# Hybrid mixer and mixture-of-experts layer on one core: where the cache rows are turned and stored, and the order of work between the output projection and the first expert product

## The chip, the cores and the metric

The kernel runs on one core of a Trainium2 chip. The metric is the device time of one execution in microseconds (us), as the median of several runs.

## What is computed

One decoder layer for a prompt of 256 tokens and a sample group of 8 x 4 tokens, T = 288 rows of D = 1024 in fp32, and a final norm.

```
xn   = rmsnorm(x) * g_mix
proj = xn @ w_in                       # columns: B gate | C gate | h | v, 512 each
u    = C * h;  z_c = B * dwconv3(u)    # last 2 rows of u per sequence are outputs (new_conv)
z_p  = scale * GroupLinear(trailing_mean_w(v) - v), w in (2, 4, 8, 16)
                                       # last 15 rows of v per sequence are outputs (new_pool)
x1   = x + concat(z_c, z_p) @ w_out
xf   = rmsnorm(x1) * g_ffn
logits = xf @ router_w + router_b;  top 4 of 32;  gates = softmax(top 4)
for e in 32 experts:  gu = xf @ w1[e] + b1[e];  gate = min(gu_left, 7);  lin = clip(gu_right, -7, 7)
                      x1 += gates[:, e] * ((gate * sigmoid(1.702 * gate) * (lin + 1)) @ w2[e] + b2[e])
y    = rmsnorm(x1) * g_final
```

The experts' weights are 32 x 12.6 MB, about 400 MB in all, and each is read once.

## The kernel before

Every engine has its own program with semaphores between them. The order of the work is written out by hand. TensorE's program goes through these stages.

**Input projection (L567 to L628).** x is turned onto partitions. Each of x and w_in is split into a high part (ACT, L955) and a low part (DVE for x, POOL for w_in, L1540), and one block (128 rows of w_in by 512 columns) is 4 x 3 products of 128x128 by 288 columns (L625 to L627). There are four groups of 8 blocks: v, C, h, B, into banks 4 to 7, 0 to 3, 4 to 7, 0 to 3. ACT may be three blocks ahead at most (`w_mix_used`). At block 0 of the second group TensorE broadcasts the rms factor over partitions by products of ones with a diagonal (L594); DVE copies it out (L1245) and then scales v, forms the trailing sums (L1262 to L1272) and C (L1277). When h is done, DVE makes u (L1282) and the convolution (L1291 to L1297). At block 2 of the last group (L599 to L606) TensorE turns the last rows of u and v, the caches, into banks 4 to 7; ACT copies them to `cache_rows` (L987 to L990) and issues 11 stores between its high parts (L1006). At block 6 TensorE makes the four pool products (L613, L614), after `cache_read`, since they write the same banks.

**Output projection (L631 to L649).** 16 blocks of the same kind, w_out's low part from POOL (L1546). As the columns of x1 are done, DVE adds x (L1334, `x1_ready`) and ACT squares (L1027, `x1_sq_ready`).

**Router (L652 to L660).** For each of 8 column blocks m of x1, one product with the router's weights (L656), written to partition group m % 3 of bank 7, and one of ones with the squares (L659), always to partition group 3. They are fp32. ACT copies the partial sums (L1029) and six small products with `pick_logits` (L673) add up the groups and turn them.

**Gate and first gather (L662 to L688, L892 to L900).** TensorE turns x1 back to rows (L666) into the banks of `TURNED_BANKS`. ACT copies the left half (L1033), and scales it into x_norm, three tiles of the left half, then exp, then copy, then three of the right half (L1036, L1047). DVE makes logits, the top 4, `mask`, then waits for exp, makes `combine` with its reciprocal, waits for the ranks (TensorE, L682, L684), and makes rank and `place`, the one-hot matrix of slots of a pair of experts. `gather_first` (L714) picks the rows of a pair by products with `place`: three pieces of 2, 2 and 4 column blocks (`FIRST_PIECES`). ACT copies each with the gain (L1056, `first_read`).

**Experts.** They go in 16 pairs, 64 slots for each expert of a pair, one period of each engine's program per pair. A period has 8 first products (L757; 4 units i of two j) for its own pair, and 2 units of second products (L779) for the pair before it; a unit is 4 MB in one of four ring slots. `add_b1` (L692) and `add_b2` (L700) start the banks with the biases, `turn_back` is L736, `gather` L710, `turn_gathered` L728, `turn_hidden` L745, and spreading back to tokens is L801 and L802. Each unit's last product signals `used`, and SyncE's queue loads a slot again when its unit has been used (L427 for w1, L432 for w2). In the first two pairs nothing is spread back; pair 1's period has the first second products (198.99 us in the trace), then ACT's `high_y` and DVE's `low_y` (L1420). `work` is one scratch buffer: `cache_rows` lies where `y_low` is written.

The change moves lines of these functions; what it touches follows with the line numbers of the profile.

Of the kernel before, what the change touches and what calls it, by code (L numbers as in the profile page):

```python
# [53 lines left out]
def hybrid_moe_layer(nc, x_prompt, x_sample, state_conv, state_pool, norm_mix_g, w_in, conv_w,  # L54
# [30 lines left out]
    with ctx:  # L85
# [129 lines left out]
        last_at = KD * T  # L215
        u_last = flat_n[:, last_at:last_at + KC * NB * CB].rearrange("p (k n) -> p k n", k=KC)
        v_last = flat_n[:, last_at + KC * NB * CB:last_at + KC * (NB * CB + NS)].rearrange("p (k n) -> p k n", k=NG)
        assert last_at + KC * (NB * CB + NS) <= NTILE * D

# [15 lines left out]
        FIRST_PIECES = ((0, 1), (2, 3), (4, 5, 6, 7))  # L235
        FIRST_BANKS = (7, 6, 4)
# [287 lines left out]
        def _(pe):  # L524
            mm = nc.tensor.matmul

            def keep_awake(times, moving):

                for _ in range(times):
                    mm(psum[:, 6, 0:moving.shape[-1]], ident[:], moving, start=True, stop=True)  # L530
# [22 lines left out]
            for j in range(4):  # L553
# [8 lines left out]
                for k in range(KD):  # L562
# [27 lines left out]
                    if j == 1 and k == 0:  # L590
# [6 lines left out]
                    if j == 3 and k == 2:  # L597


                        pe.wait_ge(last_ready, 1)  # L600
                        for i in range(KC):
                            nc.tensor.transpose(psum[0:CB, 4, i * P:(i + 1) * P], u_pad[:, i, NP:NP + CB], ident[:])
                            nc.tensor.transpose(psum[0:NB * CB, 5, i * P:(i + 1) * P], u_last[:, i, :], ident[:])
                            nc.tensor.transpose(psum[0:PB, 6, i * P:(i + 1) * P], v_pad[:, i, NP:NP + PB], ident[:])
                            last = nc.tensor.transpose(psum[0:NS, 7, i * P:(i + 1) * P], v_last[:, i, :], ident[:])
                        last.then_inc(cache_ready, 1)  # L606
                    if j == 3 and k == 6:

                        pe.wait_ge(pooled, 1)
                        pe.wait_ge(cache_read, 1)  # L610
# [19 lines left out]

            pe.wait_ge(z_pool_low_ready, NG)  # L631
            for i, (k, n) in enumerate(OUT_BLOCKS):
# [16 lines left out]
                last.then_inc(w_mix_used, 1)  # L649


            pe.wait_ge(router_ready, 1)  # L652
            for m in range(KD):
                pe.wait_ge(x1_ready, max(m + 1, KC))
                g = m % 3
                mm(psum[g * E:(g + 1) * E, 7, 0:T], router_g[:, m, :], x1_t[:, m, :], start=(m < 3), stop=(m >= KD - 3),  # L656
                   skip_group_check=True)
                pe.wait_ge(x1_sq_ready, m + 1)
                last = mm(psum[3 * E:4 * E, 7, 0:T], ones[:, 0:E], x1_sq[:, m, :], start=(m == 0), stop=(m == KD - 1),  # L659
                          skip_group_check=True)  # L660
# [17 lines left out]
            for t in REST_ORDER:  # L678
                turn_x1(1, t)

# [6 lines left out]
            def add_b1(h, b):  # L687

                pe.wait_ge(picked_b1, 2 * h + b + 1)
                for c in range(W1N):  # L690
# [58 lines left out]
            def first_product(h, b, i, j, first=False):  # L749
# [5 lines left out]
                for c in range(W1N):  # L755
                    for e in range(2):
# [47 lines left out]
            def period(h, b, first=False, spreads=True, final=False):  # L804
# [8 lines left out]
                else:  # L813
                    add_b1(h, b)
# [3 lines left out]
                for i in range(2):  # L818
                    for j in range(2):
                        first_product(h, b, i, j, first)  # L820
# [3 lines left out]
                        if second and i + j == 0:  # L824
                            pe.wait_ge(gt_read, 2)
                            turn_hidden(h, b)
                        if direct and j == 1 and i == 0:
                            pe.wait_ge(x_norm_ready, NTILE + 1)
                            pe.wait_ge(x_rest_copied, 1)
                            gather_first(1)  # L830
                            pe.wait_ge(first_read, 2)
                        if direct and i == 1 and j == 0:
                            pe.wait_ge(x_norm_ready, 2 * NTILE)
                            pe.wait_ge(x_rest_copied, NTILE)
                            gather_first(2)
# [5 lines left out]
                if direct:  # L841
                    pe.wait_ge(first_read, 3)
# [739 lines left out]
```

## Time and profile before

| | us |
|---|---|
| median of 3 runs | 1062.56 (1062.09 to 1066.23) |
| the profiled execution | 1058.53 |
| its span, first to last instruction | 1056.8 |
| TensorE busy / its weight loads | 999.4 / 414.0 |
| VectorE (DVE) busy | 290.3 |
| ScalarE (ACT) busy | 175.9 |
| GpSimd (POOL) busy | 75.4 |
| HBM read / written | 418.62 MB / 1.49 MB |

A row of the timeline gives the start in us, the duration, engine, line and operation, out<-in, and how many records it merges; in brackets the idle time before it and what ended it. A product in fp32 leaves two records, one in the split form (fp32r) and a transpose leave one. PE is TensorE, PEclk its granted clock as a share of 2.4 GHz. SPq is the queue on which SyncE issues loads.

### The profile page before, as it was taken

To read this page: it belongs to the slowest core of one execution; us is meant where nothing else is said; L and a number is where in the kernel's file an instruction comes from. 1 tells how busy PE (TensorE), PEld (TensorE's weight loads), DVE (VectorE), ACT (ScalarE), POOL (GpSimd) and SP (SyncE) were. 2 spreads that over 40 slices of the span, in tenths; PEclk is the share of its full clock that TensorE was granted. 3 is DMA by queue.
4 is the path that set the end of the run, shared out by engine and by line. 5 is a ranking of instruction groups with operands and counts; after the bars stand their busy time and mean duration, and the time that the engine had idled before them with its cause. 6 is when DMAs were issued, how large, how long until landed. Compare 5 with 4: busy or idle time off the path is not lost.

```text
span 1056.8 us, 11523 instructions
## 1 busy us (share of the span) xinstructions
PE 999.4 (95%) x4640; PEld 414.0 (39%) x4640; DVE 290.3 (27%) x510; ACT 175.9 (17%) x369; POOL 75.4 (7%) x63
## 2 busy tenths in 40 slices
PE   8999899999999999999999999999999999999886
PEld 8999433333333333333333333333333333333232
DVE  5886220222222221212222222213122222212133
ACT  5355311101010101102010101011020101011012
POOL 5866000000000000000000000000000000000001
PEclk9999899999999999999999999999999999999998
DMA  9954789999999999999999999999999999999993
GB/s 346 338 216 160 281 358 398 409 428 430 427 427 428 429 428 431 427 428 429 428 430 429 427 427 430 429 430 427 428 429 428 431 428 428 428 428 428 426 416 140
DMA packets 37904, 420.35 MB, mean 398 GB/s; under 512 B 5020, under 2 KB 5568, under 8 KB 12777
## 3 DMA queue, kind: packets, MB, share of 16 engines
q1 hardware_dynamic: 37400, 418.82, 94.6%
q10 hardware_dynamic: 473, 1.12, 0.3%
q8 instruction: 19, 0.31, 0.1%
q14 instruction: 12, 0.10, 0.0%
HBM read 418.62 MB, written 1.49 MB: 398 GB/s over the span
## 4 chain that ended last, share of the span: by engine, by line
PE 60%; DMA 34%; POOL 2%; ACT 1%; issue 1%; DVE 1%; SPq 1%; POOLq 0%; DVEq 0%; ACTq 0%
DMA ring<-in_exp_w 33%; PE psum L757 27%; PE psum L779 13%; PE psum L710 8%; PE psum L728 1%; PE psum L625 1%; PE psum L627 1%; PE psum L626 1%; PE psum L718 1%; POOL w_low L1540 1%; PE psum L801 1%; PE psum L644 1%; PE psum L646 1%; PE psum L645 1%; POOL w_out_low L1546 1%
## 5 line engine op out<-in xcount | busy, mean ns | idle before, releaser
L757 PE MATMUL psum<-ring,work 128*64 128x512 f32 x2048 | 464.3, 599 | 26.8 <-DMA ring<-in_exp_w 25.9
L757 PEld LDWEIGHTS psum<-ring,work 128*64 128x64 f32 x2048 | 137.8, 137 | 297.1 <-issue 259.1
L779 PE MATMUL psum<-ring,work 128*64 128x512 f32 x1024 | 226.1, 595 | 9.2 <-DMA ring<-in_exp_w 8.6
L779 PEld LDWEIGHTS psum<-ring,work 128*64 128x64 f32 x1024 | 75.3, 137 | 148.5 <-issue 147.0
L1402 DVE TENSOR_SCALAR work<-psum 128x512 f32<-128x512 f32 x32 | 20.6, 686 | 315.1 <-PE psum L757 315.1
L1390 DVE TENSOR_TENSOR x_acc<-x_acc,psum 128x512 f32<-128x512 f32 (+1 forms) x90 | 57.5, 678 | 180.6 <-PE psum L802 180.6
L710 PE MATMUL psum<-x_norm,place 128*128 128x512 f32 x180 | 90.0, 626 | 0.0
L1069 ACT ACTIVATE work<-psum 128x512 f32<-128x512 f32 x30 | 17.9, 597 | 389.6 <-PE psum L710 389.6
L1554 POOL TENSOR_TENSOR x_norm<-x_acc,gain 128x512 f32<-128x512 f32 x2 | 2.6, 1280 | 940.3 <-DVE x_acc L1460 940.2
L1420 DVE SCALAR_TENSOR_TENSOR y_low<-psum,gate_of,y_high 128x512 fp32r<-128x512 f32 x32 | 24.0, 751 | 145.7 <-ACT y_high L1094 144.9
L1094 ACT ACTIVATE y_high<-psum,gate_of 128x512 fp32r<-128x512 f32 x32 | 22.0, 688 | 205.3 <-PE psum L779 203.5
L1056 ACT ACTIVATE work<-psum,vecs 128x128 f32<-128x128 f32 x128 | 35.0, 382 | 120.4 <-PE psum L728 98.9
L710 PEld LDWEIGHTS psum<-x_norm,place 128*128 128x128 f32 x180 | 29.1, 187 | 60.6 <-issue 60.6
L1540 POOL TENSOR_TENSOR w_low<-ring,w_high 128x512 fp32r<-128x512 f32 x31 | 44.9, 1460 | 19.9 <-ACT w_high L955 19.2
L625 PE MATMUL psum<-x_parts,w_high 128*128 128x288 f32 x128 | 38.7, 302 | 2.4 <-DVE w_low L1219 1.3
L801 PE MATMUL psum<-y_high,back 128*128 128x512 f32 (+1 forms) x90 | 39.0, 433 | 0.0
L627 PE MATMUL psum<-x_parts,w_low 128*128 128x288 f32 x128 | 37.7, 295 | 0.0
L626 PE MATMUL psum<-x_parts,w_high 128*128 128x288 f32 x128 | 37.7, 295 | 0.0
L955 ACT ACTIVATE w_high<-ring 128x512 fp32r<-128x512 f32 x48 | 30.1, 632 | 37.8 <-PE psum L627 28.3
L802 PE MATMUL psum<-y_low,back 128*128 128x512 f32 (+1 forms) x90 | 35.5, 394 | 0.0
L1086 ACT ACTIVATE work<-work 128x512 f32<-128x512 f32 x32 | 19.6, 629 | 89.9 <-DVE work L1402 89.9
L1412 DVE SCALAR_TENSOR_TENSOR work<-psum,work 128x512 f32<-128x512 f32 x32 | 31.3, 1055 | 0.0
(208 smaller groups left out, 632.1 us busy)
## 6 DMA issues: line engine op xcount, KB each, us to landing
ring<-in_exp_w SPq DMA_DIRECT2D x186, 2048.0 KB, 25.2
ring<-in_exp_w SPq DMA_DIRECT2D x10, 1024.0 KB, 26.9
ring<-in_w_in SPq DMA_DIRECT2D x3, 2048.0 KB, 19.1
ring<-in_w_out SPq DMA_DIRECT2D x1, 4096.0 KB, 13.2
ring<-in_w_in SPq DMA_DIRECT2D x4, 512.0 KB, 7.8
ring<-in_exp_w SPq DMA_DIRECT2D x4, 512.0 KB, 23.3
x_acc<-in_x_prompt SPq DMA_DIRECT2D x2, 512.0 KB, 4.1
out<-x_norm SPq DMA_DIRECT2D x4, 256.0 KB
```

The costliest lines, as they stand in the source:

```text
L625: mm(out, w_h, x_h, start=(k == 0), stop=False, skip_group_check=True)
L626: mm(out, w_h, x_l, start=False, stop=False, skip_group_check=True)
L627: last = mm(out, w_l, x_h, start=False, stop=(k == KD - 1), skip_group_check=True)
L710: last = mm(psum[:, 6 + c, :], place[0:rows[t], t], x_norm[0:rows[t], t, c * BANK:(c + 1) * BANK], start=(t == 0), stop=(t == NTILE - 1))
L757: last = mm(psum[e * SLOTS:(e + 1) * SLOTS, c, :], gathered_t[:, b, 2 * i + j, e, :], ring_w1[:, slot, e, j, c * BANK:(c + 1) * BANK], sta ...
L779: last = mm(psum[e * SLOTS:(e + 1) * SLOTS, y_bank + c, :], h_t[:, 4 * i + j, e, :], ring_w2[:, slot, e, j, c * BANK:(c + 1) * BANK], star ...
L801: mm(psum[0:rows[t], 6 + j % 2, :], z, y_high[:, c, :], start=True, stop=False)
L802: mm(psum[0:rows[t], 6 + j % 2, :], z, y_low[:, c, :], start=False, stop=True).then_inc(spread, 1)
L1056: return A(gathered_t[:, b, k], src.rearrange("p (e n) -> p e n", e=2), ACT.Copy, scale=vecs[:, G_OWN + k:G_OWN + k + 1])
L1390: V.tensor_tensor(x_acc[0:rows[t], t, c * BANK:(c + 1) * BANK], x_acc[0:rows[t], t, c * BANK:(c + 1) * BANK], psum[0:rows[t], 6 + j % 2, : ...
L1412: V.scalar_tensor_tensor(out=gate_act[:, c, :].rearrange("p (j q) -> p q j", j=4), in0=psum[:, 2 + c, :].rearrange("p (q j) -> p q j", j=4 ...
L1540: G.tensor_tensor(w_low[:, c // KD, c % KD, :], w_in_sb[:, c // KD, c % KD, :], w_high[:, c % 3, :].bitcast(F32), ALU.subtract).then_inc(w ...
```

## The change

- The turns of the cache rows leave the input projection. DVE copies the last rows into compact scratch (`u_first`, `u_last`, `v_first`, `v_last`, now in `work` and `ramp`). In pair 1's period, after the first half (j = 0) of its unit i = 1, TensorE multiplies them with the identity, in four column groups of bank 5; ACT copies them, POOL issues the 11 stores, and DVE waits for `cache_stored` before `low_y` of that period. `add_b2` of that period waits for `cache_read`.
- The rms broadcast moves from block 0 to block 2 of the second group.
- The router's products for the first four column blocks stand before the last block of the output projection; routes use partition groups 0 and 1, squares 2 and 3.
- ACT's exp comes after the first norm. DVE makes rank, place and the maximum before the reciprocal. TensorE has 5 and 3 more dummy products.
- The first gather is in two pieces of one column block, in banks 7 and 3; the biases of banks 0 and 1 are added before it, of bank 2 after it, of bank 3 inside the first product.

```diff
@@ buffers
+        last_at = 6 * D + 768
+        u_last = flat_work[:, last_at:last_v].rearrange("p (k n) -> p k n", k=KC)
+        v_first = flat_work[:, last_v:last_s].rearrange("p (k n) -> p k n", k=NG)
+        v_last = flat_work[:, last_s:last_s + NG * NS].rearrange("p (k n) -> p k n", k=NG)
+        u_first = ramp[:, 0:KC * CB].rearrange("p (k n) -> p k n", k=KC)
-        FIRST_PIECES = ((0, 1), (2, 3), (4, 5, 6, 7))
-        FIRST_BANKS = (7, 6, 4)
+        FIRST_PIECES = ((0,), (1,), (2, 3), (4, 5, 6, 7))
+        FIRST_BANKS = (7, 3, 6, 4)
+        CACHE_BANK = 5
@@ TensorE, input projection
-                    if j == 1 and k == 0:
+                    if j == 1 and k == 2:
                         pe.wait_ge(diag_ready, 1)
...
-                    if j == 3 and k == 2:
-                        pe.wait_ge(last_ready, 1)
-                        for i in range(KC):
-                            nc.tensor.transpose(psum[0:CB, 4, i * P:(i + 1) * P], u_pad[:, i, NP:NP + CB], ident[:])
-                            nc.tensor.transpose(psum[0:NB * CB, 5, i * P:(i + 1) * P], u_last[:, i, :], ident[:])
-                            nc.tensor.transpose(psum[0:PB, 6, i * P:(i + 1) * P], v_pad[:, i, NP:NP + PB], ident[:])
-                            last = nc.tensor.transpose(psum[0:NS, 7, i * P:(i + 1) * P], v_last[:, i, :], ident[:])
-                        last.then_inc(cache_ready, 1)
                     if j == 3 and k == 6:
                         pe.wait_ge(pooled, 1)
-                        pe.wait_ge(cache_read, 1)
+                        pe.wait_ge(proj_read, 3)
+                        pe.wait_ge(last_ready, 1)
@@ TensorE, output projection and router
+            def route(m):
+                g = m % 2
+                pe.wait_ge(x1_ready, m + 1)
+                mm(psum[g * E:(g + 1) * E, 7, 0:T], router_g[:, m, :], x1_t[:, m, :], start=(m < 2), stop=(m >= KD - 2),
+                   skip_group_check=True)
+            def add_square(m):
+                g = 2 + m % 2
+                pe.wait_ge(x1_sq_ready, m + 1)
+                return mm(psum[g * E:(g + 1) * E, 7, 0:T], ones[:, 0:E], x1_sq[:, m, :], start=(m < 2),
+                          stop=(m >= KD - 2), skip_group_check=True)
...
+                if i == len(OUT_BLOCKS) - 2:
+                    pe.wait_ge(router_ready, 1)
+                    pe.wait_ge(x1_ready, KC)
+                    for m in range(KC):
+                        route(m)
+                        add_square(m)
-            for m in range(KD):
-                pe.wait_ge(x1_ready, max(m + 1, KC))
-                g = m % 3
...
+            route(KC)
+            for m in range(KC, KD):
+                if m + 1 < KD:
+                    route(m + 1)
+                last = add_square(m)
             last.then_inc(logit_parts_ready, 1)
...
             for t in REST_ORDER:
                 turn_x1(1, t)
+            keep_awake(5, ident[:], bank=7)
@@ TensorE, experts
+            def turn_caches():
+                def turn(rows_out, columns):
+                    return mm(rows_out, columns, ident[:], start=True, stop=True, skip_group_check=True)
+                pe.wait_ge(last_ready, 2)
+                for i in range(KC):
+                    own = slice(i * P, (i + 1) * P)
+                    turn(psum[0:CB, CACHE_BANK, own], u_first[:, i, :])
+                    turn(psum[32:32 + NB * CB, CACHE_BANK, own], u_last[:, i, :])
+                    turn(psum[64:64 + PB, CACHE_BANK, own], v_first[:, i, :])
+                    last = turn(psum[96:96 + NS, CACHE_BANK, own], v_last[:, i, :])
+                last.then_inc(cache_ready, 1)
...
                 for c in range(W1N):
+                    if late and c == W1N - 1:
+                        pe.wait_ge(first_read, 2)
+                        add_b1(h, b, (c,))
...
-                    add_b1(h, b)
+                    add_b1(h, b, (2,))
                     pe.wait_ge(first_read, 1)
...
+                        if second and i == 1 and j == 0:
+                            turn_caches()
...
+                    if second:
+                        pe.wait_ge(cache_read, 1)
                     add_b2(h, b)
...
                 if isinstance(r, int):
+                    pe.wait_ge(bias_step, 6)
+                    pe.wait_ge(x_half_copied, 2)
+                    pe.wait_ge(x_norm_ready, 2)
+                    add_b1(0, 0, range(2))
+                    keep_awake(3, ident[:], bank=7)
                     pe.wait_ge(x_norm_ready, NTILE)
                     pe.wait_ge(place_ready, 1)
                     gather_first(0)
-                    pe.wait_ge(bias_step, 6)
+                    pe.wait_ge(most_read, 1)
+                    gather_first(1)
                     pe.wait_ge(x_half_copied, NTILE)
-                    pe.wait_ge(most_read, 1)
@@ ACT
-            act.wait_ge(cache_ready, 1)
-            A(cache_rows[0:CB], psum[0:CB, 4, :], ACT.Copy)
...
-            for i, (dst, src) in enumerate(stores):
-                nc.scalar.dma_start(dst, src).then_inc(cache_stored, 16)
+            for i in range(3 + NB):
...
-            for t in range(NTILE):
-                norm_x(0, t)
+            norm_x(0, 0)
             act.wait_ge(shifted_ready, 1)
             A(shifted[:], shifted[:], ACT.Exp).then_inc(exp_ready, 1)
+            norm_x(0, 1)
+            norm_x(0, 2)
             copy_half(2)
...
+            def copy_caches():
+                act.wait_ge(cache_ready, 1)
+                for at_row, n in ((0, CB), (32, NB * CB), (64, PB), (96, NS)):
+                    last = A(cache_rows[at_row:at_row + n], psum[at_row:at_row + n, CACHE_BANK, :], ACT.Copy)
+                last.then_inc(cache_read, 1)
...
                     copy_hidden_t(h, b)
+                if isinstance(h, int) and h + b == 1:
+                    copy_caches()
@@ DVE
+            V.tensor_copy(v_first, v_pad[:, :, NP:NP + PB])
+            V.tensor_copy(v_last.rearrange("p k (b t) -> p k b t", b=NB), tails(v_pad, PS, PL, PB)).then_inc(last_ready, 1)
...
+            V.tensor_copy(u_first, u_pad[:, :, NP:NP + CB])
+            V.tensor_copy(u_last.rearrange("p k (b t) -> p k b t", b=NB), tails(u_pad, CS, CL, CB)[:, :, :, NT - CB:NT]).then_inc(last_ready, 1)
...
             then(V.tensor_reduce(denom[:], combine[:, :, 0:E], AX.X, ALU.add))
+            dve.wait_ge(ranks_ready, 1)
+            then(V.scalar_tensor_tensor(out=rank[:, :, 0:E],
...
+            build_place(0, 0, 0)
+            V.reduce_max(most[:], psum[:, 3, 256 + NTILE * E:256 + (NTILE + 1) * E], AX.X).then_inc(most_read, 1)
             V.memset(denom[32:64, 2:3], 1.0)
...
+                if isinstance(h, int) and h + b == 1:
+                    dve.wait_ge(cache_stored, 16 * (3 + NB))
                 if not first:
                     low_y(h, b)
@@ POOL, behind the rms of the router
+            pool.wait_ge(cache_read, 1)
+            nc.gpsimd.dma_start(new_conv_prompt[0, 0], cache_rows[0:CB]).then_inc(cache_stored, 16)
...
+            for b in range(NB):
+                nc.gpsimd.dma_start(new_pool_sample[0, b, PB - NT:PB, :],
+                                    cache_rows[96 + b * NT:96 + (b + 1) * NT]).then_inc(cache_stored, 16)
```

## Rows read from the trace of the kernel before

**Rows 1.** The page, parts 1 and 2: busy time, and the span in 40 slices

```profile
PE 999.4 (95%) x4640; PEld 414.0 (39%) x4640; DVE 290.3 (27%) x510; ACT 175.9 (17%) x369; POOL 75.4 (7%) x63
...
DMA  9954789999999999999999999999999999999993
```

**Rows 2.** Stretches of time: busy per engine, then clock, DMA share, GB/s

```profile
170.00:172.00 2.00, 2.00 (x12) 0.62 (x10) 0.69 (x2) 0.00 (x0) 0.00 (x0) 1.00 0.59 131
190.00:192.00 2.00, 2.00 (x12) 0.71 (x10) 0.00 (x0) 0.00 (x0) 0.00 (x0) 1.00 0.87 336
192.00:194.00 2.00, 2.00 (x11) 0.49 (x7) 0.00 (x0) 0.00 (x0) 0.00 (x0) 1.00 0.83 279
200.00:1000.00 800.00, 765.44 (x3328) 268.04 (x3326) 178.46 (x303) 94.78 (x214) 0.00 (x0) 1.00 1.01 428
```

**Rows 3.** Timeline of SyncE's queue: start, duration, line, load

```profile
190.80 23.62 SPq L427 DMA_DIRECT2D ring<-in_exp_w  x8
```

**Rows 4.** Timeline of TensorE in the last group of the input projection

```profile
58.61 0.29 PE L627 MATMUL psum<-x_parts,w_low 128*128 128x288 f32 x1
58.74 0.27 PE L602 MATMUL psum<-ident,ring 128*2 128x128 f32 x1
...
60.40 0.38 PE L625 MATMUL psum<-x_parts,w_high 128*128 128x288 f32 x1
```

**Rows 5.** Timelines of TensorE, POOL and DVE in the projections

```profile
27.09 1.04 PE L594 MATMUL psum<-gain,ones 128*128 128x128 f32 x6 [0.23 <-DVE ring L1242]
...
32.26 19.15 POOL L1540 TENSOR_TENSOR w_low<-ring,w_high 128x512 fp32r<-128x512 f32 x11 [0.32 <-ACT w_high L955]
...
55.84 1.22 DVE L1282 TENSOR_TENSOR ring<-psum,x_acc 128x1024 f32<-128x1024 f32 x1 [5.71 <-PE psum L627]
...
73.37 0.37 PE L644 MATMUL psum<-z_pool_parts,w_high 128*128 128x288 f32 x1 [0.48 <-POOL w_out_low L1546]
```

**Rows 6.** Groups of instructions from 99.5 to 104 us

```profile
L659 PE MATMUL psum<-work,ones 128*32 128x288 f32 x16 | 4.1, 408 | 0.0
L656 PE MATMUL psum<-ring,router_g 128*32 128x288 f32 x16 | 3.1, 418 | 0.0
```

**Rows 7.** Timeline from the gate to the first weight product

```profile
106.24 2.07 ACT L1036 ACTIVATE x_norm<-psum,rms 128x512 f32<-128x512 f32 x2
...
109.01 0.27 ACT L1047 ACTIVATE shifted<-shifted 128x96 f32<-128x96 f32 x1
...
109.63 2.94 ACT L1036 ACTIVATE x_norm<-psum,rms 32x512 f32<-32x512 f32 x3
...
110.97 0.56 DVE L1381 TENSOR_TENSOR place<-slot_id,rank 128x384 f32<-128x384 f32 x1
...
111.68 3.31 PE L718 MATMUL psum<-place,x_norm 128*128 128x128 f32 x12 [1.99 <-ACT x_norm L1036]
...
116.06 1.97 PE L757 MATMUL psum<-ring,work 128*64 128x512 f32 x4
```

**Rows 8.** Stretches of 1 us, columns as in rows 2

```profile
112.00:113.00 1.00, 1.00 (x6) 0.66 (x4) 0.86 (x7) 0.57 (x1) 0.00 (x0) 0.60 1.13 463
...
119.00:120.00 1.00, 1.00 (x6) 0.28 (x4) 0.00 (x0) 0.00 (x0) 0.00 (x0) 0.99 1.03 442
```

**Rows 9.** Timeline of TensorE: the same operations at full clock

```profile
7.42 1.50 PE L530 MATMUL psum<-ident 128*128 128x128 f32 x12
...
124.53 2.18 PE L718 MATMUL psum<-place,x_norm 128*128 128x128 f32 x12
127.42 3.65 PE L757 MATMUL psum<-ring,work 128*64 128x512 f32 x16 [0.71 <-ACT work L1056]
```

**Rows 10.** Timelines of DVE and TensorE at the turn to pair 2

```profile
212.91 1.55 DVE L1420 SCALAR_TENSOR_TENSOR y_low<-psum,gate_of,y_high 128x512 fp32r<-128x512 f32 x2 [8.68 <-ACT y_high L1094]
...
218.15 0.51 PE L801 MATMUL psum<-y_high,back 128*128 128x512 f32 x1
```

**Rows 11.** The page, part 6: DMA issues, KB each, median us to landing

```profile
ring<-in_exp_w SPq DMA_DIRECT2D x186, 2048.0 KB, 25.2
```

More of the change, by code:

```diff
@@ L525, in _, with keep_awake @@
             mm = nc.tensor.matmul
-            def keep_awake(times, moving):
+            def keep_awake(times, moving, bank=6):
                 for _ in range(times):
-                    mm(psum[:, 6, 0:moving.shape[-1]], ident[:], moving, start=True, stop=True)
+                    mm(psum[:, bank, 0:moving.shape[-1]], ident[:], moving, start=True, stop=True)
             pe.wait_ge(consts_made, 1)
@@ L686, in _, with add_b1 @@
             last.then_inc(ranks_ready, 1)
-            def add_b1(h, b):
+            def add_b1(h, b, banks=range(W1N)):
                 pe.wait_ge(picked_b1, 2 * h + b + 1)
-                for c in range(W1N):
+                for c in banks:
                     own = slice(2 * E * (c % 2), 2 * E * (c % 2 + 1))
@@ L747, in turn_hidden, with first_product @@
                     last.then_inc(h_t_ready, 1)
-            def first_product(h, b, i, j, first=False):
+            def turn_caches():
[9 more added lines that the diff above has]
+                last.then_inc(cache_ready, 1)
+            def first_product(h, b, i, j, first=False, late=False):
                 at_unit = i if first else (4 if b else -2) + i
@@ L819, in period @@
                     for j in range(2):
-                        first_product(h, b, i, j, first)
+                        first_product(h, b, i, j, first, late=direct and i + j == 0)
                         if spreads and 2 * i + j < 3:
@@ L983, in _ @@
             nc.scalar.dma_start(new_pool_sample[0][:, 0:PB - NT, :], state_pool[0][:, NT:PB, :]).then_inc(stored, 16)
[L984 to L991 removed]
+            high_parts(6, 4 * KD)
             act.wait_ge(z_pool_ready, 1)
@@ L1020, in _ @@
                             last.then_inc(bias_step, 1)
-            high_parts(IN_BLOCKS + 2 + len(stores), IN_BLOCKS + len(OUT_BLOCKS))
+            high_parts(IN_BLOCKS + 5 + NB, IN_BLOCKS + len(OUT_BLOCKS))
             for m in range(KD):
@@ L1051, in _ @@
                 norm_x(1, t)
-            act.wait_ge(cache_stored, 16 * (3 + NB))
             nc.scalar.dma_start(gain[:], final_norm_g[None, :].to_broadcast([P, D])).then_inc(g_final_landed, 16)
@@ L1334, in _, with own, build_place @@
                 V.tensor_tensor(x1_t[:, m, :], psum[:, mix_bank(m), 0:T], x_raw[:, m, :], ALU.add).then_inc(x1_ready, 1)
+            def own(table, pair):
+                return table[:, :, bass.ds(pair * 2, 2)].unsqueeze(3).to_broadcast([P, NTILE, 2, SLOTS])
+            def build_place(h, b, pair):
+                if not (isinstance(h, int) and h + b == 0):
+                    dve.wait_ge(gated_ready, 2 * h + b)
+                ids = slot_id[:].unsqueeze(1).unsqueeze(1).to_broadcast([P, NTILE, 2, SLOTS])
+                V.tensor_tensor(place[:], ids, own(rank, pair), ALU.is_equal).then_inc(place_ready, 1)
             dve.wait_ge(logits_ready, 1)
@@ L1368, in _ @@
             dve.wait_ge(combine_ready, 1)
-            dve.wait_ge(ranks_ready, 1)
-            then(V.scalar_tensor_tensor(out=rank[:, :, 0:E],
-                                        in0=psum[:, 3, 256:256 + NTILE * E].rearrange("p (t e) -> p t e", t=NTILE),
-                                        scalar=1.0, in1=mask[:, 0:NTILE, :], op0=ALU.add, op1=ALU.mult))
-            def own(table, pair):
-                return table[:, :, bass.ds(pair * 2, 2)].unsqueeze(3).to_broadcast([P, NTILE, 2, SLOTS])
-            def build_place(h, b, pair):
-                if not (isinstance(h, int) and h + b == 0):
-                    dve.wait_ge(gated_ready, 2 * h + b)
-                ids = slot_id[:].unsqueeze(1).unsqueeze(1).to_broadcast([P, NTILE, 2, SLOTS])
-                V.tensor_tensor(place[:], ids, own(rank, pair), ALU.is_equal).then_inc(place_ready, 1)
             def build_gated(h, b, pair):
@@ L1468, in round_of @@
                     dve.wait_ge(slot_step, r)
[L1469 to L1472 removed]
+                    build_place(h0, 0, 0)
                 build_gated(h0, 0, 0)
```

51 lines of the change are left out of this document (17 added, 34 removed).

## The prediction

> **What bounds the kernel now.** I read four views in this order. The page first: TensorE is busy 95% of the span, and from the eighth slice on the DMA engines stand at nine tenths or more [rows 1]. Both look full, so I asked which is waited for. The stretches of time answer it: from 200 to 1000 us the DMA share is 1.01 at 428 GB/s, while TensorE has 34.6 us without work [rows 2]. From about 200 us on the kernel is a stream of expert weights at a fixed rate, and nothing that TensorE saves there moves the end. Before that the ring of four slots is full and the stream stands still until TensorE frees one: the share is 0.59 at 170 to 172 us and 0.87 and 0.83 at 190 to 194 [rows 2]. The last gap ends with the load that the queue of SyncE issues at 190.80, when TensorE has used unit i=2 of pair 1 [rows 3]. The units issued after it come faster than the 9.8 us that the stream needs for 4 MB (two experts, at 428 GB/s), so there is no later gap. So the end of the kernel is the time of that release plus a constant. Each us by which TensorE reaches it earlier is a us of the whole, and so is each us put in front of it. The rest is a sum over TensorE's path up to 190.8 us.
>
> **Cache rows out of the input projection.** Gone from the third block of the last column group are 16 transposes; they stand between 58.74 and 60.40 [rows 4]. TensorE is paced by itself there, with the next weights ready, so 1.66 us go. What is late next: the output projection starts at 73.37, released by POOL's low part of the first w_out block [rows 5]. That chain begins with the four pool products on TensorE, which move by the same 1.66, so nothing is lost. The four ACT copies and 11 store issues also leave ACT, whose work is hidden in both kernels.
>
> **The rms broadcast two blocks later.** Its six records take 1.04 us at 27.09 [rows 5]. They are not removed. Blocks 0 and 1 of group 1 run 1.04 earlier and the DVE chain behind the broadcast starts about 3.2 later. But in this group POOL makes the low parts, 11 in 19.15 us, 1.74 each against TensorE's 1.6 a block (12 records 0.13 us apart [rows 4, 5]), and TensorE waits for it. The lead is spent there: I take 0.1 us, bounds 0 and 1.04. The later DVE chain has cover: DVE sits idle 5.71 us before 55.84 [rows 5], of which 3.2, less a moved copy of 1.3, is used. Without that cover each us would delay z_pool_low and so the output projection one for one.
>
> **Router products.** Today 16 products follow the output projection, all squares on one group of 32 columns, the routes beside them. The 16 records of squares have 4.1 us busy and the 16 of routes 3.1 in the same 4.1 us: the squares run one behind another at 0.25 us, and the routes are hidden [rows 6]. After the change both kinds are spread over two groups each. The first eight products now stand before the last block: each group has 4 records, 1.0 us if all four groups run at once, 2.0 if only two do, as rows 6 show. After the last block the path is that block's own: DVE's last x1 ends about 0.65 us behind it, ACT's square at 1.1, the last product at 1.7. So 4.1 becomes 1.7 + 1.0 to 2.0, plus 0.2 for the extra turn: a gain of 1.2 to 0.2. I take 1.1, as the first routes start within 0.01 us of each other.
> The Trainium skill, TensorEngine Tiling (Array Packing), section Key Properties, has it that different tiles load weights and multiply in parallel, but that a change of tiling mode drains the engine. By that the upper end holds, less two drains; the sum above doesn't use it.
>
> **Gate, ranks, first gather.** ACT now: two norms from 106.24, a third, the exp at 109.01, the right half's norms from 109.63 for 2.94 us [rows 7]. The exp waited behind three norms; DVE's mask was ready before. Place follows at 110.97 and the first gather at 111.68 (12 records, 3.31 us), then four b1 products and the products of weights at 116.06 [rows 7]. After the change the exp stands behind one norm, at about 107.5, and DVE builds ranks and place before the reciprocal. What ends last for place is then ranks_ready at 109.7, so place is done at 110.55 in place of 111.53. TensorE fills its gaps: 5 dummy products (six took 1.50, so 1.25 [rows 9]) behind the turns, two b1 products and 3 dummies (0.75) behind the ranks, until about 110.95. A first gather of one piece needs six records: 1.1 us by the later 12 in 2.18 [rows 9], so it ends at 112.05. But now ACT is late: its norms end at 112.9 (0.35 later, the exp having made it idle), then a copy of 0.4. The weight products start at 113.4, not 116.06: 2.7 us.
> The clock: it falls to half after the two lulls, 0.60 at 112 to 113, and is back at 119 to 120 [rows 8]. So 3.31 is a time at half clock for the greater part, and the first two blocks take from 116.06 to 124.53, 8.5 us, against 2 x 3.65 = 7.3 at full clock [rows 7, 9]. The lulls of 1.3 and 2.0 us before it are nearly filled after the change, so I take full clock: 7.3 and 0.25 for the fourth bank's b1 inside it, a further 0.95. Together 3.65, less 0.15 for more turns between array shapes: **3.5 us**. With the clock falling as before, the blocks would end at 123.6 and the gain be 0.9.
> Pieces 2 to 4 wait for ACT and DVE exactly as before. Copy of the left half and gain's load are later or earlier by under 1 us and nobody waits.
>
> **Cache rows in pair 1.** 16 products in fp32, two records each, stand before the 190.8 release, so they cost in full. 32 records at the 0.109 of the transposes [rows 4] are 3.5 us one behind another; four column groups at once make it 0.9; as full-array records of 0.18 [rows 9] it would be 5.8. I take 1.3, near the low end, for the order goes round the four groups; 0.4 of it is for the two turns between array shapes.
> ACT's four copies (below 1.1 each [rows 7]) fall between 175.5 and 180, where ACT has nothing until 184, and add_b2's new wait for them comes at 198.6: free. The stores go to POOL's queue, empty then. DVE's new wait stands before low_y, which runs at 212.91 and lets TensorE spread at 218.15 [rows 10]; behind it on DVE are the additions of pair 0's outputs. It is covered by some 35 us.
>
> **Sum.** 1.66 + 0.1 + 1.1 + 3.5 - 1.3 = **5.1 us**, taken as 5.0. Against the profiled execution (1058.5 us, span 1056.8 and 1.7 around it) that gives 1053.5. The median of the runs is 4.0 above that execution, so 1057.6 for the median.
>
> **Rivals.**
> 1. The clock falls all the same. For it: it fell though TensorE worked for 1.1 us between the lulls. Against: only ACT's wait of half a us is left. Gain 5.0 - 2.6 = 2.4: 1060.2.
> 2. Four column groups don't run at once. For it: rows 6 show two at a time, and no row four. Router gain 0.2, caches 3.5: 5.0 - 0.9 - 2.2 = 1.9: 1060.7.
> 3. Slower: the stores land late. The rows land through POOL's queue beside a full weight stream. Were each issue to take 1.3 us and the last land 25.2 us after it, as a 2 MB load does [rows 11], they'd be done at 178.5 + 14.3 + 25.2 = 218. TensorE would be held from 216.6 on, yet the stream starves only 6.7 us later, since 4 units are queued until 231.6 and the next is issued at 222.9. It costs from a landing at 223.3 on and makes the kernel slower than before from 228.4 on; at 235, 1064.3.
> The Trainium skill, SBUF — State Buffer, section "SBUF: two separate sides", warns of just this move: a DMA issued from GpSimd has its descriptors written by GpSimd, and a DVE copy between SBUF tensors shuts it out; one of 620 ns then took about 3100. By that figure, an estimate, 11 stores take up to 34 us and land near 213 or later, still before 223. No row of before shows a store from POOL.
> 4. The gain is there and the stream's rate varies by as much: 1062.
>
> **Numbers.** Forecast 0.62 (gain 3.7 to 6.7), rival 1 0.13, rival 2 0.14, rival 3 0.03, rival 4 0.08. Range: the most that the rows allow is 1.66 + 1.04 + 1.2 + 3.7 - 0.9 = 6.7, with 1.4 for the stream and the median's own scatter 1054.5; below, rivals 1 and 2 lie inside 1061.5. What a measurement can tell from no change is 0.5%, 5.3 us, and the forecast stands just under it: faster 0.43, same 0.53, slower 0.04.
>
> **What would show it.** After: no transposes in the last input block group and the output projection starting near 71.7; the last router product some 1.7 us behind it; clock 1.00 through 105 to 120; the first weight product near 110.5 in its own time; 32 small records of 1.3 us near 168; the last DMA gap ending near 186 to 187. Wrong would be a gap in the stream after 200 us, DVE waiting for cache_stored, or the first blocks at half clock.

## The result and the profile after

The changed kernel takes 1056.15 us (median of 5 runs, 1053.37 to 1056.43) against 1063.32 for the kernel before: ratio 0.9932, 95% interval 0.9913 to 0.9951. A second comparison of the same two kernels (e9) gave 0.995, 0.9932 to 0.9969. The profiled execution of after is 1053.37 us, its span 1051.6, against 1058.53 and 1056.8: 5.2 us less. The forecast was 1057.6 and 5.0. One execution each of e2 (2306 us) and e4 (1698 us) fell out of line and is left out of the ratios, not of the medians below.

The release that ends the last gap of the stream has moved from 190.80 [rows 3] to 185.75, by 5.05 us. Timeline of SyncE's queue, after:

```profile
163.91 8.83 SPq L436 DMA_DIRECT2D ring<-in_exp_w  x4
185.75 23.61 SPq L431 DMA_DIRECT2D ring<-in_exp_w  x8
```

The stretches of time of after, with the columns of rows 2: the same last gap, 5 us earlier, and then the same full stream.

```profile
184.00:186.00 2.00, 2.00 (x12) 0.71 (x10) 0.00 (x0) 0.00 (x0) 0.00 (x0) 1.00 0.81 336
186.00:188.00 2.00, 2.00 (x12) 0.62 (x10) 0.00 (x0) 0.00 (x0) 0.00 (x0) 1.00 0.85 185
...
200.00:1000.00 800.00, 765.43 (x3326) 267.79 (x3322) 174.45 (x298) 94.23 (x212) 0.00 (x0) 1.00 1.01 428
```

Where the 5.05 us came from is read from TensorE's timeline of after. It answers to rows 4, 5, 7 and 9:

```profile
65.26 0.60 PE L608 MATMUL psum<-x_acc,work 128*128 128x256 f32 x2
...
96.44 0.43 PE L629 MATMUL psum<-ring,router_g 128*32 128x288 f32 x1
96.44 0.43 PE L635 MATMUL psum<-work,ones 128*32 128x288 f32 x1
96.45 0.43 PE L629 MATMUL psum<-ring,router_g 128*32 128x288 f32 x1
96.45 0.43 PE L635 MATMUL psum<-work,ones 128*32 128x288 f32 x1
...
97.54 0.40 PE L651 MATMUL psum<-z_conv_parts,w_high 128*128 128x288 f32 x1
...
101.05 0.66 PE L675 MATMUL psum<-ident,ring 128*128 128x128 f32 x4
...
107.46 0.94 PE L534 MATMUL psum<-ident 128*128 128x128 f32 x6
108.23 2.13 PE L728 MATMUL psum<-place,x_norm 128*128 128x128 f32 x12
...
110.72 2.79 PE L784 MATMUL psum<-ring,work 128*64 128x512 f32 x12
...
113.88 4.51 PE L784 MATMUL psum<-ring,work 128*64 128x512 f32 x20
118.32 2.18 PE L728 MATMUL psum<-place,x_norm 128*128 128x128 f32 x12
```

| stage on TensorE | before | after | gained | forecast |
|---|---|---|---|---|
| start to the pool products | 66.92 | 65.26 | 1.66 | 1.76 |
| pool products to x1 turned back | 36.72 (to 103.64) | 35.79 (to 101.05) | 0.93 | 1.1 |
| to the end of the first two blocks | 20.89 (to 124.53) | 17.27 (to 118.32) | 3.62 | 3.5 |
| to the release | 66.27 | 67.43 | -1.16 | -1.3 |
| sum | | | 5.05 | 5.1 |

The first row is less exact than it looks. The first product of the input projection starts at 10.18 in before and at 10.38 in after; from there to the pool products it is 56.74 and 54.88 us, so 1.86 less.

The clock did not fall (answering to rows 8):

```profile
112.00:113.00 1.00, 1.00 (x8) 0.29 (x4) 0.08 (x1) 0.00 (x0) 0.00 (x0) 1.00 0.93 356
119.00:120.00 1.00, 1.00 (x7) 0.77 (x6) 0.00 (x0) 0.00 (x0) 0.00 (x0) 1.00 1.29 229
```

ACT's timeline: the exp stands between the norms, the right half's norms begin at 107.51, the first copy at 110.28. No wait of TensorE for ACT shows before the first weight product: from 106.02 to 120.5 its timeline has none, and the second piece of the gather and a b1 product stand in front of 110.72. Only the load of weights ahead of that product waited 0.2 us for ACT. So both were ready at nearly the same time.

```profile
103.65 1.17 ACT L1058 ACTIVATE x_norm<-psum,rms 128x512 f32<-128x512 f32 x1
104.94 0.28 ACT L1068 ACTIVATE shifted<-shifted 128x96 f32<-128x96 f32 x1
...
107.51 2.96 ACT L1058 ACTIVATE x_norm<-psum,rms 32x512 f32<-32x512 f32 x3
110.28 0.57 ACT L1078 ACTIVATE work<-psum,vecs 128x128 f32<-128x128 f32 x2
```

### The profile page after: what moved, and what is told of

It is laid out like the page before. It is cut to its first block, busy times and chain, and to the rows that moved or that the text cites. A ratio compares the mean times of both kernels' runs of the same rounds, so it can differ in the third digit from the quotient of the medians.

```text
span 1051.6 us, 11593 instructions
## 1 busy us (share of the span) xinstructions
PE 997.9 (95%) x4672; PEld 413.8 (39%) x4672; DVE 291.5 (28%) x512; ACT 176.2 (17%) x369; POOL 81.7 (8%) x74
## 4 chain that ended last, share of the span: by engine, by line
PE 61%; DMA 33%; POOL 2%; DVE 1%; issue 1%; ACT 1%; SPq 0%; POOLq 0%; DVEq 0%; ACTq 0%
DMA ring<-in_exp_w 33%; PE psum L784 27%; PE psum L806 13%; PE psum L720 8%; PE psum L738 1%; PE psum L620 1%; PE psum L622 1%; PE psum L621 1%; POOL w_low L1574 1%; PE psum L728 1%; PE psum L828 1%; PE psum L651 1%; PE psum L653 1%; PE psum L652 1%; POOL w_out_low L1580 1%
## 5 line engine op out<-in xcount | busy, mean ns | idle before, releaser
L784 PE MATMUL psum<-ring,work 128*64 128x512 f32 x2048 | 463.3, 597 | 27.1 <-DMA ring<-in_exp_w 26.2
```

The source lines that it names most:

```text
L784: last = mm(psum[e * SLOTS:(e + 1) * SLOTS, c, :], gathered_t[:, b, 2 * i + j, e, :], ring_w1[:, slot, e, j, c * BANK:(c + 1) * BANK], sta ...
```

## Experiments

TensorE reaches the pool products at times that differ by up to 4 us between executions: 65.1 to 69.2 in these kernels, whose work up to there is all but the same (e8 alone still has the transposes). So each experiment is read by the time from the pool products to the release: 123.88 us before (190.80 - 66.92), 120.49 after (185.75 - 65.26). It repeats well: 120.48, 120.44, 120.45 and 120.50 in four other runs that leave this stretch alone (e9, e6, e7, e5).

The release is not yet the end. The last time that TensorE waits for a landing of weights for a first product shows what reached the end of the stream: it ends at 997.98 in before, at 992.61 in after (its row stands under "The scatter of the runs"), and at 995.07 in e3. The rows of before and of e3:

```profile
997.98 7.09 PE L757 MATMUL psum<-ring,work 128*64 128x512 f32 x32 [2.71 <-DMA ring<-in_exp_w]
995.07 7.09 PE L784 MATMUL psum<-ring,work 128*64 128x512 f32 x32 [2.69 <-DMA ring<-in_exp_w]
```

| | pool products to the release | pool products to the last wait for weights |
|---|---|---|
| before | 123.88 | 931.06 |
| changed kernel, and e5, e6, e7, e9, e10 | 120.44 to 120.50 | 927.27 to 927.47 |
| e8, gate part alone | 120.22 | 927.37 |
| e1, no dummies | 123.65 | 930.90 |
| e4, caches twice | 121.32 | 928.35 |
| e2, router behind | 119.53 | 926.12 |
| e3, caches later | 119.27 | 926.88 |
| e11, e2 and e3 together | 118.39 | 926.29 |
| e12, e11 with tail dummies | 118.40 | 926.40 |

Release and last wait lie 806.6 to 807.3 us apart, but 807.6 to 808.0 in the three kernels with the caches turned later.

### Is it the dummies or the order? (e1)

```diff
-            keep_awake(5, ident[:], bank=7)
...
-                    keep_awake(3, ident[:], bank=7)
```

> The changed kernel without its 5 and 3 dummy products before and after the ranks. Theory A, the dummies hold the clock: without them the granted clock falls to half near 110 us as it did before at 112.6, for some 6 us, and the release that ends the last gap of the stream (185.75 in the changed kernel) comes 2.2 to 2.6 later, near 188.1; span about 1054. Rival B, the shorter lulls that the reordering leaves are enough: clock 1.00 throughout, release at 185.6 to 185.8, span 1051.6.

From the pool products to the release it took 123.65 us (191.38 - 67.73), 3.16 more than the changed kernel; median 1059.36, ratio to before 0.9968 (0.9945 to 0.9991). The clock fell near 112.5, as in rows 8, and was half until 119:

```profile
112.00:113.00 1.00, 1.00 (x7) 0.66 (x5) 0.90 (x5) 1.00 (x3) 0.00 (x0) 0.74 1.12 459
113.00:114.00 1.00, 1.00 (x3) 0.44 (x5) 1.00 (x3) 0.34 (x1) 0.00 (x0) 0.50 0.90 381
118.00:119.00 1.00, 1.00 (x5) 0.10 (x1) 0.00 (x0) 0.00 (x0) 0.00 (x0) 0.50 0.88 377
```

and the first 12 records of weight products took 5.39 us for 2.79:

```profile
108.43 0.49 PE L691 MATMUL psum<-mask,before 128*128 128x128 f32 x2 [1.26 <-DVE mask L1397]
...
110.62 2.32 PE L727 MATMUL psum<-place,x_norm 128*128 128x128 f32 x12 [0.68 <-DVE place L1374]
...
113.59 5.39 PE L783 MATMUL psum<-ring,work 128*64 128x512 f32 x12
...
119.51 4.51 PE L783 MATMUL psum<-ring,work 128*64 128x512 f32 x20
```

Theory A stands, and more so than expected: beside the new order, eight dummies carry 3.16 of the stage's 3.62 us. The dummies in the old order were not run, so what they are worth without the reordering is not shown. The reordering alone starts the weight products 2.3 us earlier (9.56 us behind the small logit products, against 11.86 before), but at half clock, where 1.9 of it is lost again. Even lulls of 1.3 and 0.7 us, shorter than before, let it fall.

### The gate part alone (e8)

The kernel before with exp, rank, place, pieces, b1 products and dummies as in the changed kernel, nothing else.

> The kernel before with the gate's part of the change alone: exp behind one norm, ranks and place first, first gather in two pieces, the b1 products around it, 5 and 3 dummies. Theory A, parts add up: the release of 190.80 moves by the 3.6 that this stage gained, to 187.2, clock 1.00, span near 1053.2. Rival B, the stage gained only because what stands before it had moved: less than 3 us.

The release came at 189.45 and the pool products at 69.23: 120.22, so 3.66 less than before, against 3.62 within the whole change. Median 1057.57, ratio 0.9966 (0.995 to 0.9981). The clock was full from 104 to 124 us. The parts add up.

### The router's half inside the output projection (e2)

```diff
-                if i == len(OUT_BLOCKS) - 2:
-                    pe.wait_ge(router_ready, 1)
-                    pe.wait_ge(x1_ready, KC)
-                    for m in range(KC):
-                        route(m)
-                        add_square(m)
...
-            route(KC)
-            for m in range(KC, KD):
-                if m + 1 < KD:
-                    route(m + 1)
+            pe.wait_ge(router_ready, 1)
+            pe.wait_ge(x1_ready, KC)
+            for m in range(KD):
+                route(m)
                 last = add_square(m)
```

> The changed kernel with all 16 router products behind the output projection again, but routes still on two column groups and squares on two. Theory A, the gain of 1.0 comes from the spread over four groups, and the half inside the output projection only costs a second turn between array shapes: 8 products take 1.0, the rest end by ACT's last square, so the logits come 0.5 to 0.8 earlier than in the changed kernel; release near 185.1. Rival B, having half inside is what pays: the stage takes about 4 us again and the release is 1.0 later, near 186.8.

From the pool products to the release 119.53 (188.55 - 69.02), 0.96 less than the changed kernel; median 1054.65, ratio 0.9917 (0.989 to 0.9944). All 16 products stand in 2.08 us, from 101.74 to the next at 103.82, four at once:

```profile
101.74 0.43 PE L629 MATMUL psum<-ring,router_g 128*32 128x288 f32 x1
101.74 0.43 PE L635 MATMUL psum<-work,ones 128*32 128x288 f32 x1
101.75 0.43 PE L629 MATMUL psum<-ring,router_g 128*32 128x288 f32 x1
101.76 0.43 PE L635 MATMUL psum<-work,ones 128*32 128x288 f32 x1
102.00 0.41 PE L629 MATMUL psum<-ring,router_g 128*32 128x288 f32 x1
...
103.82 0.66 PE L669 MATMUL psum<-ident,ring 128*128 128x128 f32 x4
```

So the gain is the spread over four groups, worth 1.9. The half that stands inside the output projection takes half of it back: 97.54 - 96.34 = 1.2 us there with its turns, while what is left behind the last block still takes 1.8, waiting for ACT's squares. In e2 the 2.1 us of products behind the block cover those squares.

### The cache rows (e3, e4, e6)

Turned one unit later, behind the unit that releases the load:

```diff
-                        if second and i == 1 and j == 0:
-                            turn_caches()
...
                 first_product(h, b, 2, 1, first)
+                if second:
+                    turn_caches()
                 first_product(h, b, 3, 0, first)
```

> The changed kernel with the cache rows turned one unit later in pair 1, behind the product whose end releases the load of 185.75. Theory A, only what stands before that release costs: it comes at 184.6, 1.16 earlier, no new gap (the next release is 9.2 behind it, under the 9.8 of a unit), span near 1050.4. Rival B, the next gap opens instead, since the start of a load takes about 2 us and 9.2 is close to 9.8: the stream's share dips at 194 to 197 and up to 1.16 is given back, span 1051.6.

119.27 (187.46 - 68.19): 1.22 less, so the release moved as theory A has it. The stream did not keep it. Its share at 194 to 198 is 1.03 and 0.99, but from 198 to 202, where the changed kernel moves 434 and 426 GB/s, it moves less:

```profile
198.00:200.00 2.00, 2.00 (x12) 0.63 (x10) 2.00 (x4) 0.53 (x1) 0.00 (x0) 1.00 1.02 392
200.00:202.00 2.00, 2.00 (x12) 0.67 (x10) 2.00 (x3) 0.00 (x0) 0.00 (x0) 1.00 1.02 350
```

The last wait for weights ends 0.47 us earlier than in the changed kernel and not 1.22 (table above): 0.75 is given back, as rival B has it. The next release is issued at 196.71, 9.25 behind the first, where it was 8.01 behind in the changed kernel (193.76). That the dip comes from this release and not from the stores, which also moved to 190 to 197, is likely by the order of time and not shown. The median, 1056.09 (ratio 0.9944, 0.9922 to 0.9965), shows neither.

Made twice:

```diff
-                for i in range(KC):
+                for i in (0, 1, 2, 3, 0, 1, 2, 3):
```

> The changed kernel with the 16 cache products made twice, same banks and same data. Theory A: the release comes 0.9 later (32 more records at four times 0.11 for each round of four), near 186.65, and the span is 0.9 longer, 1052.5: each us before the release is a us of the whole. Rival B, the stream has slack there that hides it: span unchanged.

121.32 (186.92 - 65.60): 0.83 more, for 32 records in four groups, 0.104 us for each round of four. Of the 1.16 that the first 32 cost, 0.33 is then left for the two turns between array shapes. The last wait for weights ends 1.00 later. The span was 1056.4 and the median 1059.49 (ratio 0.9977, 0.9958 to 0.9996), 3.3 us above the changed kernel's first median. The release gives 0.8 of them and the clock of the last pair 2.6 in this profile; why the timed runs are that much longer each time stays open.

Stores on ACT's queue:

```diff
                 last.then_inc(cache_read, 1)
+                act.wait_ge(cache_read, 1)
+                for dst, src in stores:
+                    nc.scalar.dma_start(dst, src).then_inc(cache_stored, 16)
```

> The changed kernel with the 11 stores of cache rows issued by ACT behind its copies in place of POOL. Theory A, the stores are covered by over 20 us either way: release at 185.75, low_y near 207.9 as now, span 1051.6 within 0.3. Rival B, the stores through POOL's queue cost the weight stream (another queue and its descriptors): span shorter by 0.5 to 1.

120.44, and a median of 1056.69 (ratio 0.9952, 0.9937 to 0.9967): no difference. The rival of late stores is out. In the changed kernel POOL issues the 11 stores in 5.9 us, the last some 0.5 us apart; the page has them landing 5.6 to 9.8 us after their issue (POOLq in its part 6), by about 187, and low_y runs at 207.94:

```profile
171.05 0.77 POOL L1585 DMA_DIRECT2D out<-work  x1 [67.43 <-ACT work L1108]
...
172.84 4.10 POOL L1590 DMA_DIRECT2D out<-work  x8
```

The Trainium skill (SBUF — State Buffer, section "SBUF: two separate sides") gives about 3100 ns for a DMA that is issued from GpSimd under a DVE tensor_copy. That was not met here, with 0.5 to 0.8 us an issue. But DVE was busy for only 1.42 of these 5.89 us, so this case hardly tests it.

### Is TensorE or the stream the bound from 200 us on? (e5)

```diff
                 if not (first or second):
+                    keep_awake(4, ident[:], bank=7)
                     turn_hidden(h, b)
```

> The changed kernel with 4 dummy products (1.0 us) in each of the 14 periods from pair 2 on, 14 us of work for TensorE in all. Theory A, from 200 us on only the stream is waited for: TensorE's wait for weights shrinks by about the same 14 us, span within 1 us of 1051.6. Rival B, TensorE at 95% busy is the bound: span up to 14 us longer.

120.50 to the release, median 1056.61 (ratio 0.9952, 0.9935 to 0.9968), as the changed kernel. TensorE's waits for weights (in total, times, longest), first with the dummies, then without:

```profile
PE psum L784 <- DMA ring<-in_exp_w: 14.7, 20, 2.7
PE psum L806 <- DMA ring<-in_exp_w: 7.6, 10, 0.9
```

```profile
PE psum L784 <- DMA ring<-in_exp_w: 26.2, 34, 2.7
PE psum L806 <- DMA ring<-in_exp_w: 8.0, 10, 0.8
```

11.5 us of the waits for in_exp_w went (26.2 - 14.7), filled by work for nothing, and neither the time nor the last landing moved: from the pool products to the last wait for weights it is 927.37 us, against 927.35. TensorE, 95% busy there, was not the bound.

### The rms broadcast (e7)

```diff
-                    if j == 1 and k == 2:
+                    if j == 1 and k == 0:
```

> The changed kernel with the rms broadcast back at block 0 of the second group. Theory A, POOL's low parts set that stage, so the move is worth 0 to 0.2: release at 185.75 to 185.95. Rival B, the six products came off TensorE's path by the move: release 1.0 later, 186.8.

From the first product of the input projection to the pool products it took 54.81 us (65.62 - 10.81), against 54.88 (65.26 - 10.38) in the changed kernel. The move is worth nothing; the 0.1 us was not there. In both orders TensorE waits three times for POOL's low parts between 35 and 43 us, for up to 0.62 us, as the prediction had it.

### The scatter of the runs, and a better version (e9 to e12)

Timed runs of one kernel lie 3 to 6 us apart. Two places in the profiles differ between executions. At the start, TensorE waits for x_prompt for up to 1.9 us, and in e1 and e8 the first products then come at half clock. And in the last pair TensorE waits 2.7 and 2.9 us, and the clock falls there in some executions and not in others. The changed kernel's first profile and the one of e9, same program:

```profile
992.61 7.09 PE L784 MATMUL psum<-ring,work 128*64 128x512 f32 x32 [2.70 <-DMA ring<-in_exp_w]
1002.57 0.50 PE L710 MATMUL psum<-bias_parts,pick_b 64*128 64x512 f32 x2 [2.87 <-issue]
```

```profile
992.51 8.78 PE L784 MATMUL psum<-ring,work 128*64 128x512 f32 x32 [2.71 <-DMA ring<-in_exp_w]
1004.04 0.50 PE L710 MATMUL psum<-bias_parts,pick_b 64*128 64x512 f32 x2 [2.74 <-issue]
```

The releases were 185.75 and 185.72, yet the spans 1051.6 and 1053.0: the same 32 records took 1.7 us longer, in part at half clock. The span less the release is 866.0 in before and 865.9 in the first profile of after, which both kept the clock there, but 867.3 to 869.7 in all the others without dummies in the last pair. So the 5.2 between these two profiles fits the release's 5.05 in part because both happened to end undisturbed. In the kernel with caches made twice it hit the second products (16.57 us for 13.95).

> The changed kernel as it is, beside the others on one chip. Over all profiled executions so far the span less the time of the release (185.75) is 865.9 where the granted clock stays full while TensorE waits for the last pair's weights, and up to 869.5 where it falls there. Theory A, the scatter of 3 us between executions is that and the landing of x_prompt at the start: median 1056.2, so 5.5 under the kernel before. Rival B, the first comparison's 7.2 holds.

Median 1055.36 against 1061.71, ratio 0.995 (0.9932 to 0.9969): 6.4 here, 7.2 in the first comparison. The second interval reaches from 3.3 to 7.2 us and holds the forecast 5.0; the first, from 5.2 to 9.3, begins just above it. Three kernels that leave the path alone (e5, e6, e7) came to 0.9952, 0.9952 and 0.9953, which is 5.0 to 5.1 us. Theory A stands as far as this goes.

The dummies for the last pair:

```diff
+                if final:
+                    keep_awake(8, ident[:], bank=7)
                 first_product(h, b, 3, 0, first)
...
                 first_product(h, b, 3, 1, first)
+                if final:
+                    keep_awake(8, ident[:], bank=7)
```

> The changed kernel with 8 dummy products (2.0 us) twice in the last pair's period, where TensorE waits 2.7 and 2.9 us. Theory A, the half clock near 1006 comes from those waits: it stays at 1.00 to 1040, the second products take 13.95 in every execution (16.57 in the one with caches made twice), the median is 1 to 2 lower and the span less the release 865.9. Rival B, the fall has another cause or the dummies delay the products: no change or up to 2 us longer.

My theory fell: median 1060.11 (ratio 0.9985, 0.9973 to 0.9997), 4.8 above e9.

```profile
989.78 2.05 PE L534 MATMUL psum<-ident 128*128 128x128 f32 x16
992.56 7.09 PE L784 MATMUL psum<-ring,work 128*64 128x512 f32 x32 [0.73 <-DMA ring<-in_exp_w]
999.58 2.05 PE L534 MATMUL psum<-ident 128*128 128x128 f32 x16
1006.83 0.79 PE L710 MATMUL psum<-bias_parts,pick_b 64*128 64x512 f32 x2 [5.21 <-issue]
```

The first eight did what they should: the wait is filled and the 32 records take 7.09 (as they also do in some executions without dummies). But the second eight stand ahead of the loop's end and the branch on the number of rounds, and the products behind it start at 1006.83, not 1002.57. The gap that the profile calls issue is 5.21 us behind 2.05 us of dummies, where it was 2.87 in all, and then the clock falls in it. So it doesn't shrink with the work in front of it. What TensorE's program waits for there wasn't settled.

> The changed kernel with both gains of the earlier runs: router products behind the output projection in four groups (0.96) and cache rows turned behind the releasing unit (1.22). Theory A, they add: release 2.2 earlier from the pool products on (118.3 behind them against 120.49), median about 1054. Rival B, the second gap opens when the first closes: under 1.5 in all.

118.39 (183.51 - 65.12), 2.10 less than the changed kernel: on the release the two gains add. At the stream's end they don't. The last wait for weights ends 1.06 us earlier than in the changed kernel, no more than in e2 alone (1.23), so rival B holds there. Median 1054.37, ratio 0.9932 (0.9915 to 0.9949), 1.0 under e9; in its profile the clock fell twice in the last pair. It is below both kernels, but it is not told apart from e2 (1054.65, or 1054.23 without its stray execution; 0.9917) or from the changed kernel (e9), whose intervals overlap with its own. Nothing shows it better than e2; by the last wait for weights, moving the caches added nothing.

> Router products behind, cache rows later, and the dummies in the last pair's period. Theory A: the three add, median 1052.5 to 1053.5, below both kernels. Rival B, as for each part.

118.40 to the release (185.21 - 66.81), as e11. Median 1059.54 (ratio 0.9983, 0.9972 to 0.9994): the dummies behind the last unit cost here as in e10, with the same 5.21 us gap.

## Why the prediction was right

**Right.** The bound: the release decides when the last weights land. In e5 work in the place of 11.5 us of waits behind it moved nothing; in e1 and e4, with the release 3.16 and 0.83 us later, the last wait for weights ended 3.55 and 1.00 later. The medians alone would not have shown it. The limit of this rule is in e3 and e11, where of 1.22 us on the release 0.75 and more was lost again. Rms broadcast 0 for 0.1, for the reason given. Gate 3.62 for 3.5. Caches 1.16 for 1.3, and the choice near the low end, four groups at once, is what e4 measured. Stores covered. The price of the rival on late stores has a slip: by its own terms a landing at 235 gives about 1069.3 and not 1064.3. Nothing hangs on it, since the stores landed by about 187.

**Right, with some luck in it.** Input projection: 1.66 for 1.66 from the start of the span, but 1.86 from the first product, which came 0.20 later in after. And "ACT is late": the working let the weight products wait for ACT until 113.4, in the times of before. It counted one piece of the first gather, done at 112.05, and left out the second piece (1.1) and the b1 product behind it (0.25), which TensorE makes before the weight products; they too end at 113.4. In the trace TensorE doesn't wait there. The start came as forecast, 110.72 for about 110.5, with TensorE's own queue as much of a bound as ACT.

**Right in sum, with causes that don't part that way.** Read as stretches of the timeline, the terms of the gate came out in size. From x1 turned back to the first weight product 2.75 us went (12.42 and 9.67) for the forecast 2.7. The first two blocks take 7.60 us for 8.47, so 0.87 for the term "The clock" at 0.95. Read by cause, e1 parts them differently: without the dummies the stage gains 0.46, so with the new order in place the clock is 3.16. In e1 the weight products start 2.3 us earlier than in before, yet the clock is back between 119 and 119.5 in both, and most of the lead is lost under it. Of this the prediction had the size: its rival "The clock falls all the same" took 2.6 us off and left 0.9, measured 3.16 and 0.46.

**Right in sum, with a wrong part.** "Router products" came to 0.93 for 1.1. The prediction counted the half inside the output projection as part of the gain; e2 shows that it costs 0.96, and that the spread over four groups is worth 1.9. The working had both numbers: 1.0 us of products for each half and ACT's last square 1.1 us behind the block. All products behind give 2.1, less than 1.0 + 1.7 + 0.2. I didn't set the two orders side by side.

**The median.** The forecast took the profiled execution's distance of 4.0 to the median as fixed. The profile of after was 2.8 below its own median. Two sources of the scatter are known, the start and the last pair. The first comparison's 7.2 lies above the 5.0 to 6.4 of the four later ones; that the rest of it is scatter is likely and not shown.

## What to carry to other kernels

In a kernel whose stream is full from some point on, find the last gap and the instruction whose end closes it. Work in front of that instruction costs in full. Work behind it is free only as far as the next release is still early enough: moved by one unit, the cache rows gave 1.2 us on the release and less than 0.5 at the end of the stream. So follow a gain to the last landing. Where small dependent steps leave TensorE idle, price the clock first: with the new order in place, eight dummy products were worth 3.16 us, and without them that order gained 0.46.

## What the runs showed of the hardware

Four fp32 products of 128x32 run at once: 16 records of 288 columns in about 1.0 us, a round of four every 0.25 us (e2), and 32 of 128 columns in 0.83 (e4). Two changes between array shapes cost some 0.33 us together (1.16 less 0.83). The clock fell after lulls of 1.3 and 0.7 us with 1.5 us of products between them (e1). And TensorE's gap at the end of a loop and a branch was 2.4 to 3.1 us in the kernels without dummies in front of it, and 5.21 in the two with them (e10, e12).
